# A transformer stack on one core: cross-attention's scores and mixes as three products of rounded halves, the query's norm factor in the softmax's scale

## What is computed

```python
def memory_cross_attention(h, mem_n, wq, wkv, wo):
    b, s, _ = h.shape
    m = mem_n.shape[1]
    q = (h @ wq).reshape(b, s, XATTN_HEADS, XATTN_HEAD_DIM)
    kv = mem_n @ wkv
    k = kv[..., :D_MODEL].reshape(b, m, XATTN_HEADS, XATTN_HEAD_DIM)
    v = kv[..., D_MODEL:].reshape(b, m, XATTN_HEADS, XATTN_HEAD_DIM)
    scores = jnp.einsum('bshd,bmhd->bhsm', q, k).astype(jnp.float32) * (XATTN_HEAD_DIM ** -0.5)
    probs = jax.nn.softmax(scores, axis=-1).astype(v.dtype)
    o = jnp.einsum('bhsm,bmhd->bshd', probs, v).reshape(b, s, D_MODEL)
    return o @ wo
```

## Time and profile before

| what | value |
|---|---|
| median of 3 runs | 849.12 us (848.76 to 849.17) |
| the profiled execution's own time | 849.34 us |
| its span | 847.3 us |
| PE busy | 835.3 us (99%) |
| PEld, DVE, ACT, POOL busy | 766.1, 577.3, 476.9, 353.2 us |
| chain that ended last | 87% PE, 6% DVE, 3% ACT |

### The profile page before, as it was taken

The page is one execution under the profiler, slowest core; times in us unless marked ns, Lnnn a source line. Parts: engine busy times, 40 slices in busy tenths (PEclk is TensorE's granted clock), DMA queues, the critical chain, the costliest instruction groups (busy, mean ns, idle before and its releaser), DMA issues.

```text
span 847.3 us, 14837 instructions
## 1 busy us (share of the span) xinstructions
PE 835.3 (99%) x5858; PEld 766.1 (90%) x5858; DVE 577.3 (68%) x1214; ACT 476.9 (56%) x793; POOL 353.2 (42%) x173
## 2 busy tenths in 40 slices
PE   9999999999999999999999999999999999999997
PEld 4578999998899999999999988999999888888886
DVE  4789879886467896767677879686448445444445
ACT  7353345443766655555555864555447666666665
POOL 0000000001751598888887300200000788888883
PEclk9999999999999999999999999999999999999999
DMA  9998556654275556555555546364535556566651
GB/s 350 367 384 272 202 208 214 206 168 140 73 253 182 175 182 194 178 193 176 184 189 176 162 150 197 101 194 127 179 100 174 174 177 198 183 195 191 198 178 73
DMA packets 44742, 161.37 MB, mean 190 GB/s; under 512 B 5105, under 2 KB 5377, under 8 KB 43522
## 3 DMA queue, kind: packets, MB, share of 16 engines
q1 hardware_dynamic: 44384, 159.38, 58.0%
q10 hardware_dynamic: 290, 1.05, 0.3%
HBM read 159.37 MB, written 1.05 MB: 189 GB/s over the span
## 4 chain that ended last, share of the span: by engine, by line
PE 87%; DVE 6%; ACT 3%; DMA 2%; issue 1%; POOL 1%; ACTq 0%; DVEq 0%; POOLq 0%
PE bank L667 13%; PE bank L672 13%; PE bank L670 12%; PE bank L1104 9%; PE bank L1110 5%; PE bank L1193 2%; PE bank L1195 2%; PE bank L1197 2%; PE bank L1143 2%; PE bank L1141 2%; PE bank L1145 2%; DVE wlo L526 2%; PE bank L1003 2%; PE bank L769 1%; PE bank L771 1%; PE bank L775 1%
## 5 line engine op out<-in xcount | busy, mean ns | idle before, releaser
L526 POOL TENSOR_TENSOR wlo<-raw,whi 128x1024 fp32r<-128x1024 f32 (+1 forms) x147 | 334.8, 2300 | 407.2 <-ACT whi L1375 407.0
L1375 ACT ACTIVATE whi<-raw 128x1024 fp32r<-128x1024 f32 (+1 forms) x253 | 258.6, 1026 | 66.7 <-PE bank L672 22.6
L1824 DVE SCALAR_TENSOR_TENSOR accs<-bank,vec,accs 128x189 f32<-128x189 f32 (+4 forms) x440 | 161.1, 433 | 71.2 <-ACT accs L1687 71.2
L526 DVE TENSOR_TENSOR wlo<-raw,whi 128x1024 fp32r<-128x1024 f32 x106 | 129.0, 1229 | 29.1 <-ACT whi L1375 28.4
L667 PE MATMUL bank<-h,whi 128*128 128x256 f32 x504 | 143.7, 286 | 0.0
L672 PE MATMUL bank<-h,whi 128*128 128x256 f32 x504 | 142.3, 283 | 0.0
L670 PE MATMUL bank<-h,wlo 128*128 128x256 f32 x496 | 140.5, 283 | 0.7 <-DVE wlo L526 0.7
L667 PEld LDWEIGHTS bank<-h,whi 128*128 128x128 f32 x504 | 96.6, 192 | 0.7 <-issue 0.3
L672 PEld LDWEIGHTS bank<-h,whi 128*128 128x128 f32 x504 | 96.7, 192 | 0.0
L670 PEld LDWEIGHTS bank<-h,wlo 128*128 128x128 f32 x496 | 95.1, 192 | 1.1 <-DVE wlo L526 1.0
L1104 PE MATMUL bank<-h,whi 128*128 128x512 f32 x352 | 88.4, 392 | 0.5 <-DVE gl L1821 0.4
(11 more groups left out here) (362 smaller groups left out, 1851.0 us busy)
## 6 DMA issues: line engine op xcount, KB each, us to landing
raw<-in_up SPq DMA_DIRECT2D x88, 512.0 KB, 3.5
raw<-in_w_in SPq DMA_DIRECT2D x45, 512.0 KB, 4.5
raw<-in_down SPq DMA_DIRECT2D x44, 512.0 KB, 3.5
ada_sc<-in_ada SPq DMA_DIRECT2D x8, 1024.0 KB, 19.9
ada_kT<-in_adaT SPq DMA_DIRECT2D x16, 512.0 KB, 4.7
raw<-in_w_out SPq DMA_DIRECT2D x16, 512.0 KB, 4.5
raw<-in_w_in_t SPq DMA_DIRECT2D x12, 512.0 KB, 4.5
ada_sc<-in_adaT SPq DMA_DIRECT2D x8, 512.0 KB, 7.7
```

Of the source, the lines that this page charges most:

```text
L526: return e.tensor_tensor(wlo[:, j % HL, 0:k], raw[:, j % RAW, 0:k], whi[:, j % HL, 0:k].bitcast(F32), ALU.subtract)
L1375: e.activation(whi[:, j % HL, 0:(k1 - k0) * 128], raw[:, j % RAW, 0:(k1 - k0) * 128], ACT.Copy).then_inc(S.hi.up(j))
L1824: return e.scalar_tensor_tensor(out=out, in0=a, scalar=s, in1=b, op0=o1, op1=o2)
```

## The change

Scores and mixes no longer use plain fp32 products. Query, key, value and turned probabilities are each cut into a high half rounded to fp32r and a rest, as the weights are, and each plain product becomes three fp32r products (high by high, high by rest, rest by high). ACT writes the high halves: `qTh` (new, one for each wq chunk), `kTh` (new, one for each head), `PTh` and `vM` (the copies that were there, now of type fp32r). DVE writes the rests: `qTl` in the place of `qT`, and, new, `kTl` (for each head), `vMl` (two instructions for each wv pair) and `PTl` (for each head). The norm factor no longer multiplies the query: its row (`spread`, `by_row`, `rsd1`) is gone, and it enters the exponential as a scale for each partition, `rc[:, 40:42]`, and the negated maximum by `rc[:, 42:44]`.

```diff
             def scores(h):
                 slot, free = aux_ring.take(("scores", h), S.soft, h)
                 w.wait_ge(*free)
                 w.wait_ge(S.qT, 2 * h + 1)
-                w.wait_ge(S.kTs, 0)
                 for s in range(2):
-                    for i in range(2):
-                        t = e.matmul(banks[4 + slot][:, s * L:s * L + L], qT[:, 2 * h + i, s * 128:s * 128 + 128],
-                                     kT[:, 2 * h + i, :], start=i == 0, stop=i == 1)
+                    for i, (p, (q, k)) in itertools.product(range(2), enumerate(query)):
+                        t = e.matmul(banks[4 + slot][:, s * L:s * L + L], q[:, 2 * h + i, s * 128:s * 128 + 128],
+                                     k[:, 2 * h + i, :], start=i == 0 and p == 0, stop=i == 1 and p == 2)
...
             def mix(h):
-                w.wait_ge(S.PT, h)
-                w.wait_ge(S.vM, (h, 1))
+                w.wait_ge(S.PTl, h)
+                w.wait_ge(S.vMl, h)
...
-                    lin("wq", 2 * h + i, banks[slot][:, 0:L], hm, free,
-                        (lambda: spread("w_out2", aux_bank("w_out2"))) if 2 * h + i == 1 else None)
+                    lin("wq", 2 * h + i, banks[slot][:, 0:L], hm, free)
...
+            def query(n):
+                w.wait_ge(S.chunk, ch("wq", n))
+                e.activation(M["qTh"][:, n, :], lin_bank(("wq", n))[:, 0:L], ACT.Copy).then_inc(S.qh.up(n))
+
+            def key(h):
+                w.wait_ge(S.kTs, 0)
+                e.activation(M["kTh"][:, 2 * h:2 * h + 2, :], M["kT"][:, 2 * h:2 * h + 2, :],
+                             ACT.Copy).then_inc(S.kT.up(("hi", h)))
+
             for h in range(4):
+                if h:
+                    query(2 * h)
                 splits(ch("wq", 2 * h) + HL)
                 if h == 0:
                     w.wait_ge(S.total, "w_out2")
                     root("w_out2", aux_bank("w_out2")[:, 0:2])
+                    query(0)
+                key(h)
+                query(2 * h + 1)
                 splits(ch("wq", 2 * h + 1) + HL)
-                if h == 0:
-                    by_row("w_out2", M["rsd1"][:, :], aux_bank("w_out2")[:, 0:L])
                 if h == 1:
                     mem_value(1)
                 if h:
                     turn(h - 1)
...
+            def low_value(n):
+                w.wait_ge(S.vM, (n, 1))
+                cols = slice(n * 256, n * 256 + 256)
+                for m in range(2):
+                    t = stt(M["vMl"][:, m, cols], lin_bank(("wv", n))[:, m * 256:m * 256 + 256], rc("mem")[:, m:m + 1],
+                            M["vM"][:, m, cols].bitcast(F32), ALU.mult, ALU.subtract)
+                t.then_inc(S.vMl.up(n))
+
             tt(kT[:, :, :], kT[:, :, :], aux_bank("mem_row")[:, 0:L].unsqueeze(1).broadcast_to((128, 8, L)),
                ALU.mult).then_inc(S.kTs.up(0))
+            low_value(0)
             residual("w_out2")
...
+            def low_turn(h):
+                w.wait_ge(S.PT, h)
+                tt(M["PTl"][:, h % 2, :], aux_bank(("turned", h))[:, :], M["PTh"][:, h % 2, :].bitcast(F32),
+                   ALU.subtract).then_inc(S.PTl.up(h))
...
             for h in range(4):
                 for n in (2 * h, 2 * h + 1):
+                    if n % 2:
+                        w.wait_ge(S.kT, ("hi", h))
+                        keys = slice(2 * h, 2 * h + 2)
+                        tt(M["kTl"][:, keys, :], kT[:, keys, :], M["kTh"][:, keys, :].bitcast(F32), ALU.subtract)
+                    w.wait_ge(S.qh, n)
+                    tt(M["qTl"][:, n, :], lin_bank(("wq", n))[:, 0:L], M["qTh"][:, n, :].bitcast(F32),
+                       ALU.subtract).then_inc(S.qT.up(n))
                     los(ch("wq", n) + HL)
-                    w.wait_ge(S.chunk, ch("wq", n))
-                    tt(M["qT"][:, n, :], lin_bank(("wq", n))[:, 0:L], M["rsd1"][:, :], ALU.mult).then_inc(S.qT.up(n))
...
                 if 0 < h < 3:
                     los(ch("wv", 2 * h) + HL)
                     los(ch("wv", 2 * h + 1) + HL)
+                    low_value(h)
+                if h:
+                    low_turn(h - 1)
                 w.wait_ge(S.att, ("scores", h))
```

## The result

The changed kernel takes 850.32 us (median of 22 runs, 849.75 at least), the kernel before 849.20 (22 runs, 848.68 at least). The ratio is 1.0013, with a 95% interval of 1.0008 to 1.0019. So the change costs 1.1 us: the interval leaves out 1, but the difference lies within the 0.2% that was called "same". 850.0 had been forecast. One of the 22 runs of the changed kernel took 1642.81 us at a granted clock of 1.00; nothing on record explains it, the ratio leaves it out, and the median without it is 850.30.

The account below looks back on a forecast made before the run. PE, busy 835.3 of 847.3 us, was taken as the bound. Waits of 3.88 less 0.42 before and 2.53 saved gave +0.93: profiled 849.34 becomes 850.3, median 850.0 us; range 848.3 to 851.3.

Parts of the forecast that it names:

- 12 products in a block: One block of scores or mix on PE: twelve fp32r products 0.12 us apart take 1.44 us, 0.29 saved per block.
- mix(0): Mix of head 0: PE waits 0.86 us for PTl(0), which DVE makes behind vMl(1); no wait before.
- mix(1): Mix of head 1: PE waits 1.29 us for PTl(1), behind vMl(2) on DVE; only scores(2) covers the chain.
- scores(3): Scores of head 3: PE's wait grows to 0.82 us because ACT's copy qTh now comes ahead of qTl.
- mix(2): Mix of head 2: PE waits 0.91 us for PTl, behind the rounding and the wlo of wo0.
- mix(3): Mix of head 3: 2.59 us of PE work covers the 2.51 to its signal; wait 0, at most 0.14.
- scores(3) before: Scores of head 3 in the kernel before: PE waited 0.42 us for qT, subtracted from the new waits.
- The stage before: Ahead of attention: vMl(0) puts 0.76 us ahead of three wlo; PE loses nothing or a few hundredths.
- What PE saves: Attention stage on PE: eight blocks save 2.32 us and the norm factor's two transposes 0.21, 2.53 us of work.
- Rival (a): Attention stage: DVE and ACT finish the rests under scores, PE loses only 0.40 at scores(3); 847.0 us; chance 0.07.
- Rival (b): PE's plain blocks: plain fp32 products cost four fp32r products, so PE saves 4.05 us; 848.5 us; chance 0.05.
- Rival (c): At wv1b: qTh(2) ahead of ACT's rounding makes weights late (slack 0.6); 851.1 to 851.6 us; chance 0.17 includes longer waits.

Follow-up runs that it names:

- both orders and late rests: The changed kernel with PTl and PTh moved ahead of other work on DVE and ACT, and PE's products with a late operand last; 846.68 us, ratio 0.9970.
- the norm factor's: Against the kernel before, only the norm factor moved into the softmax's scale, with plain fp32 scores and mixes; 849.18 us, ratio 1.0002.
- `vMl` twice: The changed kernel with each of the four instructions that make vMl(1) and vMl(2) run again into a spare buffer; 851.76 us, ratio 1.0031.
- DVE's order alone: The changed kernel with PTl moved ahead of vMl on DVE, at head 2 also ahead of the wlo of the wv chunks; 848.80 us, ratio 0.9998.

## Why the prediction was right

The sum held term by term. Each wait is the gap between starts, and the 0.07 to 0.10 behind its first product (at scores(3), from the end of the four transposes, 0.43 after their start):

| term | predicted | measured |
|---|---|---|
| 12 products in a block | 1.44 | 1.43 |
| mix(0) | 0.86 | 0.73 + 0.10 = 0.83 |
| mix(1) | 1.29 | 1.25 + 0.08 = 1.33 |
| scores(3) | 0.82 | 621.14 - 620.38 = 0.76, + 0.07 = 0.83 |
| mix(2) | 0.91 | 0.85 + 0.07 = 0.92 |
| mix(3) | 0 (0 to 0.14) | 0.01 + 0.10 = 0.11 |
| scores(3) before | 0.42 | 620.63 - 620.29 = 0.34, + 0.07 = 0.41 |
| whole | +0.93 | +1.10 |

The measured waits sum to 4.02; less 0.41 and 2.53 that is +1.08, against +1.10 of the stage. What the forecast lacked is mostly mix(3): I took 0 from a range (0 to 0.14) whose upper part was right. Mix(3) starts 633.35 - 632.62 - 6 times 0.12 = 0.01 late, and its twelve products took 634.89 - 633.35 = 1.54, 0.10 more than twelve without a wait, though the trace puts down no idle time there. The stage before paid nothing for `vMl`(0), as forecast: the changed kernel is 0.43 us ahead at 486 us (the last section) and 578.06 - 577.62 = 0.44 ahead at 578.

- **What PE saves.** The block at 0.29 less and the transposes at 0.21 were shown apart by the kernel without waits (-2.59 in all) and by the norm factor's (-0.21). Of the -2.59, 2.53 is work and the rest the shorter wait at scores(3).
- **Rival (a), rests hidden.** It would have had no waits at the mixes; three were there. The experiment with both orders and late rests has no wait at a mix and a shorter one at scores(3), 0.32: 846.7. With the changed kernel's 0.83 there it would be 847.2, against the rival's 847.0.
- **Rival (b), plain products at four times an fp32r product.** It asks for 4.05 us saved. The kernel whose timeline is without waits at the mixes gained 2.59, and the rows of the blocks have 1.43 against 1.73. What fails is the price of a pass: the prediction took the 0.12 us of an fp32r product for it. The granted clock is 1.00, 2.4 GHz, in this stretch. By that, and this is an estimate from the rows, a plain product of 1.73 / 4 = 0.43 us is some 1040 cycles, about four for each of its 256 columns, while an fp32r product's 0.12 is 288, more than one for each. So the four passes of the Trainium skill ("FP8 and Floating Point Precision", TensorE Precision Notes) agree with the plain product's own time; it is the fp32r product that costs more than a quarter of it. How many passes the array makes, and what holds the fp32r product, no run here shows.
- **Rival (c), weights late at wv1b.** It did not come. DVE's timeline has the rest of wv1b, and PE's that chunk's first product at 591.02 (L750), in step with the ones ahead of it:

```profile
588.84 1.23 DVE L533 TENSOR_TENSOR wlo<-raw,whi 128x1024 fp32r<-128x1024 f32 x1
```

It ended at 590.07, 0.95 ahead; less the restart of 0.22 that is a slack of 0.7, where I had 0.6. The exponential takes 0.56 us (the row 586.39 above) against the 0.47 of before (the row 587.32 below): 0.09 more, inside the bound of 0.1.

The rows of DVE that priced the new work were the right ones: `PTl` has 680 ns where `ol` had 686, `vMl` 479 where `zb` had 478. (The Trainium skill, "VectorE: DVE Perf Modes", The TRN2 errata, gives (N + 151)/0.96 ns for an fp32 `tensor_tensor` addition, 691 ns for 512 columns; this subtraction, with one operand from a bank, agrees within 2%.)

## What to carry to other kernels

When a change adds an operand that another engine must make, count from the last issue that it depends on to its end through everything that stands ahead of it in that engine's list, not only through its own inputs: in three of the four waits here, instructions that `PTl` didn't need stood ahead of it. Once an engine is busy all the time, whatever is added to a chain that it already waits for costs its full time, however idle the engines on that chain are (four instructions 0.39 apart cost 1.56, with `vMl` twice); so put the rest that is waited for first on its engine, and on PE the products that don't need it first. Here the one or the other turned +1.1 us into -1.5 and -2.0, and both together into -2.5.

## What the runs showed beside this

The traces of single executions are offset against each other long before the change. ACT's timeline in the kernel before (its last row is the exponential of head 0):

```profile
12.04 1.00 ACT L1456 ACTIVATE cb<-bank 128x1024 f32<-128x1024 f32 x1
...
233.65 0.63 ACT L1375 ACTIVATE whi<-raw 128x512 fp32r<-128x512 f32 x1 [1.17 <-DMA raw<-in_w_b]
...
587.32 0.47 ACT L1784 ACTIVATE E<-bank,sm 128x256 f32<-128x256 f32 x1 [5.64 <-DVE sm L2425]
```

and in the one with DVE's order alone:

```profile
13.06 1.00 ACT L1464 ACTIVATE cb<-bank 128x1024 f32<-128x1024 f32 x1
```

ACT waited there for an input (0.44 us for `in_ctxT`, ahead of 10.96), and `cb` starts 1.02 us later, 565 us ahead of the change. The changed kernel agrees with the kernel before here (`cb` at 12.03). These two part at 235.7 us: in the kernel before, ACT waited 1.17 us for a transfer of weights (the row 233.65), and PE starts a product with a rest of weights 0.43 us after the product at 235.27, where 0.12 is the step:

```profile
235.70 0.39 PE L670 MATMUL bank<-ybh,wlo 128*128 128x256 f32 x1
```

The changed kernel has no such wait there, and has been 0.43 us ahead since (486.04 against 486.47 at the next wait that both have). So the 0.44 at the start of the stage goes with a transfer that was later in one execution, 340 us ahead of the change. In the kernel with both orders and late rests the granted clock (PEclk) was also low early on, as its busy time by stretch shows:

```profile
core 0: us, PE busy (x) PEld busy (x) DVE busy (x) ACT busy (x) POOL busy (x), PEclk, DMA share, GB/s
12.00:20.00 8.00, 7.39 (x46) 4.50 (x50) 3.49 (x9) 4.60 (x9) 0.00 (x0) 0.79 1.03 419
```

Its profiled execution took 849.18 us while its median is 846.68. Differences of a microsecond are read from a stage's own length or from medians, not from one span.
